# Moving the convolution taps, the head tiles and the last tile of a gated feed-forward to other places in VectorE's and ScalarE's order

## The reference

```python
hn = _rmsnorm(h, pre_ffn_gain[l])
gu = hn @ w_up[l]                                    # 2048 -> 2 * 5632
g = _dwconv_centred(gu[..., :D_FF], ffn_conv_w[l], ffn_conv_b[l])   # 3 taps along the tokens
u = gu[..., D_FF:]
f = (jax.nn.gelu(g, approximate=True) * u) @ w_down[l]
h = h + _rmsnorm(f, post_ffn_gain[l])
```

## Time and profile before

| | |
|---|---|
| median of 3 runs | 2573.16 us (2573.05 to 2573.49) |
| the profiled execution | 2572.96 us |
| its span, first to last instruction | 2571.2 us |
| TensorE busy in the span | 99% |
| VectorE busy | 88% |
| ScalarE busy | 59% |
| passes 1 to 3 of group 0 in the trace | 1925 to 2054 us |
| passes 1 to 3 of group 1 | 2280 to 2409 us |

### The profile page before, as it was taken

How to read it: one execution, slowest core, us unless ns; L and a number is a source line. 1 busy time by engine, 2 the same in 40 slices (tenths; PEclk the granted TensorE clock), 3 DMA queues, 4 the chain that set the end, 5 groups by cost and what they waited for, 6 DMA issues and landing times.

```text
span 2571.2 us, 30572 instructions
## 1 busy us (share of the span) xinstructions
PE 2554.5 (99%) x12114; PEld 2138.1 (83%) x12114; DVE 2253.4 (88%) x1825; ACT 1515.2 (59%) x1401; POOL 3.5 (0%) x8
## 2 busy tenths in 40 slices
PE   9999999999999999999999999999999999999998
PEld 8888888888888888888888888888888888888887
DVE  7889999999958998779998878797799987799888
ACT  6555666567646555446565566536566555465654
POOL 0000000000000000000000000000000000000000
PEclk9999999999999999999999999999999999999999
DMA  7565555555664555555555564544455645555554
GB/s 246 178 229 175 198 184 197 195 199 194 224 218 174 203 213 199 195 196 196 205 207 194 185 229 162 173 138 176 152 197 180 213 164 213 197 212 180 197 219 141
DMA packets 71923, 497.97 MB, mean 194 GB/s; under 512 B 8183, under 2 KB 9432, under 8 KB 12648
## 3 DMA queue, kind: packets, MB, share of 16 engines
q1 hardware_dynamic: 71784, 496.06, 54.8%
HBM read 493.93 MB, written 2.10 MB: 193 GB/s over the span
## 4 chain that ended last, share of the span: by engine, by line
PE 92%; DVE 4%; issue 1%; ACT 1%; DMA 1%; SPq 0%; DVEq 0%; ACTq 0%
PE acc L2905 29%; PE acc L2912 14%; PE acc L2847 9%; PE acc L2930 9%; PE acc L2924 9%; PE acc L2926 9%; PE acc L2855 5%; DVE w_lo L1606 2%; PE acc L3047 1%; ACT w_hi L870 1%; PE acc L3279 1%; PE acc L3055 1%; PE aux L3361 1%; PE aux L3420 1%; PE aux L3537 1%
## 5 line engine op out<-in xcount | busy, mean ns | idle before, releaser
L870 ACT ACTIVATE w_hi<-raw 128x2048 fp32r<-128x2048 f32 (+1 forms) x499 | 954.0, 1912 | 654.8 <-PE acc L2905 248.5
L1606 DVE TENSOR_TENSOR w_lo<-raw,w_hi 128x2048 fp32r<-128x2048 f32 (+1 forms) x499 | 1135.8, 2281 | 170.1 <-ACT w_hi L870 162.9
L2905 PE MATMUL acc<-w_hi,xa 128*128 128x512 f32 x2176 | 515.8, 389 | 0.0
L2905 PEld LDWEIGHTS acc<-w_hi,xa 128*128 128x128 f32 x2176 | 408.1, 188 | 84.7
L2912 PE MATMUL acc<-w_lo,xa 128*128 128x512 f32 x1088 | 268.8, 389 | 0.0
L2847 PE MATMUL acc<-xa,w_hi 128*128 128x512 f32 x1056 | 254.1, 393 | 0.0
L2912 PEld LDWEIGHTS acc<-w_lo,xa 128*128 128x128 f32 x1088 | 204.2, 188 | 42.4
L2847 PEld LDWEIGHTS acc<-xa,w_hi 128*128 128x128 f32 x1056 | 194.9, 188 | 39.3 <-issue 0.7
L2905 PE MATMUL acc<-w_hi,hid 128*128 128x512 f32 x768 | 182.9, 390 | 0.0
L2905 PEld LDWEIGHTS acc<-w_hi,hid 128*128 128x128 f32 x768 | 143.7, 188 | 29.8
L870 ACT ACTIVATE w_hi<-w_sum 128x2048 fp32r<-128x2048 f32 x52 | 99.9, 1920 | 111.0 <-PE acc L2905 41.3
(11 more groups left out here) (447 smaller groups left out, 3571.2 us busy)
## 6 DMA issues: line engine op xcount, KB each, us to landing
raw<-in_w_in SPq DMA_DIRECT2D x158, 1024.0 KB, 4.8
raw<-in_w_gate_up SPq DMA_DIRECT2D x88, 1024.0 KB, 4.8
raw<-in_w_down SPq DMA_DIRECT2D x88, 1024.0 KB, 4.9
raw<-in_w_up SPq DMA_DIRECT2D x87, 1024.0 KB, 4.8
raw<-in_w_out SPq DMA_DIRECT2D x32, 1024.0 KB, 4.8
raw<-in_w_uq SPq DMA_DIRECT2D x3, 1024.0 KB, 4.8
h_tok<-in_x_tok SPq DMA_DIRECT2D x1, 2048.0 KB, 9.3
raw<-in_w_ukv SPq DMA_DIRECT2D x4, 512.0 KB, 3.7
```

Of the source, the lines that this page charges most:

```text
L870: act.activation(hi_part(u, run)[:, 0:kt * P], raw_of(u)[:, 0:kt * P], ACT.Copy).then_inc(hi_made, splits(u, run))
L1606: dve.tensor_tensor(lo_part(u, run)[:, 0:kt * P], raw_of(u)[:, 0:kt * P], hi_part(u, run)[:, 0:kt * P], ALU.subtract).then_inc(lo_made, sp ...
L2905: last = pe.matmul(acc[:, bank(t + c)], a, w, start=(first and k == 0 and half == 0), stop=False, skip_group_check=more)
```

## The change

The computation stays the same; only places in two engines' orders change. `pass_taps(p - 1)` moves from form GATE_2 to form GM_6, that is from behind GM_3's remainder to behind GM_2's, the seventh form. The head's steps move: scaling from GM_5 to GM_7, middle taps and taps from GATE_2 to UP_1, gelu from GM_2 to GM_4, product from GM_7 to UP_2, the high part from UP_1 to UP_2, the low part from UP_1 to form UP_2 of pass 1. The last tile's high and low parts move from ahead of the down stage into its form PLAIN_2, behind M_5's `w_hi` and `w_lo`.

```diff
@@ ScalarE
+                def last_high(i):
+                    m = GT - 4 + i
+                    act.wait_ge(op_f32, v0 + m + 1)
+                    act.activation(hid[:, m, 0:S], tmp[:, 3], ACT.Copy).then_inc(op_hi, 1)
+
                 def last_tile(i, between=None):
...
                     act.activation(tmp[:, 2], tmp[:, 2], ACT.Gelu_apprx_tanh).then_inc(gate_out, 1)
-                    act.wait_ge(op_f32, v0 + m + 1)
-                    act.activation(hid[:, m, 0:S], tmp[:, 3], ACT.Copy).then_inc(op_hi, 1)
+                    if i < 3:
+                        last_high(i)
...
                             if p:
                                 pass_middle(p - 1)
-                            else:
-                                head_middle()
...
                         if form == GM_2:
                             if p:
                                 pass_gelu(p - 1)
-                            else:
-                                head_gelu()
                         if form == UP_1:
                             if p:
                                 pass_high(p - 1)
                             else:
-                                head_high()
+                                head_middle()
+                        if form == GM_4 and p == 0:
+                            head_gelu()
+                        if form == UP_2 and p == 0:
+                            head_high()
...
                         if p or form != PLAIN_1:
                             split(u + form + 2)
+                        if p == 0 and form == PLAIN_2:
+                            last_high(3)
@@ VectorE
-                def pass_taps(p):
-
-                    for back in (1, 0):
+                def pass_taps(p, backs=(1, 0)):
+
+                    for back in backs:
+                        if back == 0:
+                            step.wait()
                         for n in range(4):
...
-                        if back:
-                            step.wait()
...
                         if form == GM_5:
                             weight_sum(u, 3)
-                            if p == 0:
-                                head_scaled()
-                        if form == GATE_2:
-                            if p:
-                                pass_taps(p - 1)
-                            else:
-                                head_taps()
+                        if form == GM_6 and p:
+                            pass_taps(p - 1)
                         if form == GM_3:
                             weight_sum(u, 4)
...
                             if p:
                                 pass_product(p - 1)
                             else:
-                                head_product()
+                                head_scaled()
                         if form == UP_1:
+                            if p == 0:
+                                head_taps()
                             up_sum(p, GM_4, 1, 1, 4)
                             if p:
                                 pass_low(p - 1)
-                            else:
-                                head_low()
+                        if form == UP_2 and p == 0:
+                            head_product()
+                        if form == UP_2 and p == 1:
+                            head_low()
...
                 last_product(3)
-                last_low(3)
...
                         if p or form != PLAIN_1:
                             split(u + form + 2)
+                        if form == PLAIN_2 and p == 0:
+                            last_low(3)
```

## The result

| | before | changed |
|---|---|---|
| median of 5 runs | 2573.16 us (2572.72 to 2573.64) | 2585.91 us (2583.80 to 2586.88) |
| ratio | | 1.0048, 95% interval 1.0037 to 1.0059 |
| profiled execution, its span | 2572.96, 2571.2 | 2585.94, 2584.1 |

The change costs 12.75 us. The median lies inside the forecast range, 3.1 us above its point of 2582.8.

What follows compares the result with a forecast made beforehand. TensorE, busy 99%, was taken to bound the kernel, through its work plus its stalls. Passes +12.5, head -3.55 + 1.8 and last tile -1.1 gave +9.65, so 2582.8 us; range 2578.5 to 2587.0.

Steps and rivals of the forecast that it cites:

- Form 7's remainder: GM_2's w_lo, seventh in a pass: VectorE idles 2.75 us for w_hi, and TensorE's stall, costing 0.41, goes.
- a sign of being wrong: GM_2's remainder starting before 1939 us; forecast was 1939.65, behind about 2.7 us of idle VectorE.
- The taps: Eight VectorE taps in passes 1 to 3, behind GM_2's remainder: start at 1941.86 and take 3.27 us together.
- The doubt about 3.8 us: VectorE's taps: if each waited for an empty pipe, 8 x 0.475 = 3.8 us, and the sum would be +12.8.
- Form 8, and what is queued behind: GM_7, eighth in a pass: TensorE stands 2.60, loses about 2.50; UP_1 just holds; net +2.09 per pass, +12.5 for six.
- The head and the last tile: Moved steps outside the taps of passes 1 to 3: head -3.55 + 1.8, last tile -1.1 us.
- ScalarE's wait ahead of form 3: Start of pass 1: the head's high part waits for the product ahead of GM_5's w_hi; +1.1 and +0.7, sum +1.8.
- The clock: Rival: 1.2 GHz for two short forms behind each of six 2.6 us stands of TensorE, +32, 2615; chance 0.03.
- the bounds of the other terms: Passes, head and last tile at their bounds: +6.2 up to +13.5, taken together 2579.4 to 2586.7 us.
- a late form 9: Rival: UP_1, ninth in a pass, misses its remainder too; at 0.5 per pass +3, 2586; chance 0.1.
- No effect: Rival: the six later stalls stay, only head and last tile count: -2.9, 2570.3; chance 0.03.

Runs made afterwards that it cites:

- those of 4.8 us: Changed kernel with weight sum 4 directly behind the taps, ahead of GM_7's remainder, in passes 1 to 3, making TensorE's stands longer; 2606.84 us, ratio 1.0134.

## Why the prediction was right, and where it was off

- *Form 7's remainder.* Right: VectorE idle for 2.75 us, ended by ScalarE's `w_hi`, stall gone. (In pass 1 the idle time is 0.85, for the head's sake.) The prediction named as a sign of being wrong that this remainder starts before 1939, and in pass 1 it starts at 1937.48. But that limit was written in the times of the kernel before. TensorE begins form 7 at 1938.16 now, where it began at 1940.33, so the remainder starts 0.68 us ahead of it, as the forecast had it (1939.65 and 1940.33):

```profile
1938.16 0.19 PEld L2931 LDWEIGHTS acc<-w_hi,xa 128*128 128x128 f32 x1
```

- *The taps.* 3.27 forecast, 3.26 measured. TensorE's idle row is 2.62 where 2.60 were forecast. The doubt about 3.8 us is settled too.
- *Form 8, and what is queued behind.* Right. Per pass 45.16 - 43.04 = +2.12 for +2.09. Form 9 holds by 0.1 us (1994.79 and 1994.89 above); that rival is out.
- *The head and the last tile.* The mechanism right, the size 0.6 off for the head: -2.3 for -1.75 (within its bounds), and -1.1 for -1.1 for the last tile. ScalarE's wait ahead of form 3 is there. In group 0, ScalarE, then TensorE, where the earlier trace rows had no wait:

```profile
1920.61 0.75 ACT L1445 ACTIVATE hid<-tmp 128x256 fp32r<-128x256 f32 x2 [6.37 <-DVE tmp L2601]
1921.27 1.90 ACT L870 ACTIVATE w_hi<-w_sum 128x2048 fp32r<-128x2048 f32 x1
...
1923.28 0.19 PEld L2931 LDWEIGHTS acc<-w_hi,s_hi 128*128 128x128 f32 x1 [0.43 <-issue]
...
1925.55 0.76 PEld L2937 LDWEIGHTS acc<-w_lo,s_hi 128*128 128x128 f32 x4 [0.58 <-DVE w_lo L1613]
```

The view names nothing that ended the 0.43 ("issue"). That it was the wait for `w_hi` is read from the times: `w_hi` was done at 1923.17, the load starts at 1923.28, and with the high part moved behind it the wait is gone.

- *The clock.* The step that failed: the sum kept the full clock behind all six stands, and the rival was given a chance of 0.03 and 5.4 us behind each of six. It happened behind three, at 1.5 to 1.6 us each: +4.6. That is more than the 3.1 us by which the point was low; -0.8 of the opening and -0.6 of the head lie against it.
- *The range.* That the time lies inside it is in part luck. Its upper end was drawn for the bounds of the other terms and for a late form 9, which didn't happen, and not for the clock. With the half clock behind all six stands, as with those of 4.8 us, I estimate three times 1.5 to 1.6 us more, about 2590.5, which is outside.
- *No effect.* This rival is out, and its price, -2.9 for head and last tile with the taps in their old place, was wrong too; alone they measure +0.45, no difference. In the sum the term held (-3.4 for -2.9) only because VectorE's new idle time ahead of form 7's remainder absorbs the delay that the head's high part brings. The prediction doesn't mention this, so that is luck as well.

## What to carry to other kernels

When steps are moved on an engine that feeds the bounding one, write down for each operand when it is wanted and when it is ready: here TensorE lost what form 8's remainder was late, 2.1 us a pass net of the old stall, and behind half of the stands 1.5 to 1.6 us more by its clock. Work belongs where the engine idles for another's result, in pieces that fit: four taps in 2.75 us of waiting cost nothing, eight behind it cost 2.1 us a pass. And the costs of such moves don't add up: an idle stretch absorbs another step's lateness only as long as it is idle.

## What was not expected of the hardware

TensorE's clock followed its standing. In four profiles with stands of 2.6 us, 12 of 24 were followed by 3.4 us at 1.2 GHz; of those of 4.8 us six of six; of the eight of 0.9 to 2.2 us in the variants with half or all of the taps in their old place (and the head moved) none. With nine more matmuls in each stand the half clock was gone, and these 54 matmuls made the kernel 4.2 us faster. What decides between two equal stands was not found; the same kernel showed it behind the same three of six in both of its profiles, its variants behind others. The Trainium skill (TensorE: Matmul & The Clock Gate, "What's actually happening") has the clock drop after idleness and return with sustained work. The traces agree in direction: in these stages the half clock came only behind stands, and the full clock was back after 3.4 or 6.8 us.
